# Hybrid diffusion trunk layer in split fp32: where three chores stand among the matmuls, and the column order of the routed token rows

## The reference, cut to what matters

```python
h = rmsnorm(x, g_pre1) * (1 + sc1) + sh1          # modulation rows from silu(c) @ w_mod + b_mod
proj = h @ w_in                                   # input projection, then RG-LRU and attention branches
t = (ga * out_a + gb * out_b) @ w_o               # output projection, 640 x 2048 @ 2048 x 2048
x = x + g1 * rmsnorm(t, g_post1)
h = rmsnorm(x, g_pre2) * (1 + sc2) + sh2
aff = softmax(h @ w_router)                       # 16 experts
vals, idx = top_k(aff.T, cap)                     # per expert 64 latent and 16 context tokens
xs = h[idx]
hid = silu(xs @ w_gate) * (xs @ w_up)
ye = (hid @ w_down) * vals                        # added back to the tokens' rows
x = x + g2 * rmsnorm(f, g_post2)
```

## Time and profile before

| what | value |
|---|---|
| median of 3 runs | 2970.52 us |
| lowest and highest run | 2968.2 and 2975.15 us |
| profiled execution | 2973.51 us |
| its span in the trace | 2971.9 us |
| PE busy | 2853.0 us (96%) |
| DVE busy | 2189.3 us (74%) |
| mean granted PE clock | 0.981 |

### The profile page before, as it was taken

One profiled execution on the slowest core, in us unless ns is written; L12 is line 12 of the kernel. 1 busy time (PEld: TensorE's weight loads), 2 busy tenths in 40 slices (PEclk: granted clock), 3 DMA queues, 4 the chain that ended last, 5 costly groups with the idle time before them and its releaser, 6 DMA issues.

```text
span 2971.9 us, 42745 instructions
## 1 busy us (share of the span) xinstructions
PE 2853.0 (96%) x15690; PEld 2303.6 (78%) x15690; DVE 2189.3 (74%) x1948; ACT 1555.7 (52%) x1510; POOL 287.3 (10%) x341
## 2 busy tenths in 40 slices
PE   7999999999999999999999996999999999999994
PEld 3689999999999999989988774666666666666662
DVE  7639688796777777763343567888888888888886
ACT  7821212224555555542232445777777777777774
POOL 1000000002111111000000000001000101101100
PEclk8999999999999999999999997999999999999997
DMA  9668677684333333364343656999999999999996
GB/s 380 245 214 257 203 251 236 210 278 124 120 118 119 118 119 119 98 196 130 115 143 125 253 200 235 355 383 395 377 394 379 391 386 376 382 377 383 384 392 236
DMA packets 293047, 757.51 MB, mean 255 GB/s; under 512 B 20328, under 2 KB 184720, under 8 KB 228320
## 3 DMA queue, kind: packets, MB, share of 16 engines
q1 hardware_dynamic: 267168, 639.52, 59.4%
q0 software_dynamic: 23264, 101.24, 10.6%
q10 hardware_dynamic: 2544, 15.82, 1.3%
HBM read 700.61 MB, written 55.89 MB: 255 GB/s over the span
## 4 chain that ended last, share of the span: by engine, by line
PE 80%; DVE 9%; issue 4%; DMA 4%; ACT 2%; DVEq 0%; SPq 0%; ACTq 0%; POOLq 0%; POOL 0%
PE ps L483 16%; PE ps L484 16%; PE ps L485 15%; PE ps L2077 7%; PE ps L2078 7%; PE ps L2079 7%; DVE mod_acc L1419 4%; PE ps L2211 2%; PE ps L2213 2%; PE ps L2212 2%; PE ps L1981 2%; PE ps L2141 1%; DVE probs L1640 1%; DMA raw<-in_w_mod 1%; DVE w_lo L438 1%
## 5 line engine op out<-in xcount | busy, mean ns | idle before, releaser
L416 DVE TENSOR_TENSOR we_lo<-raw,we_hi 128x2048 fp32r<-128x2048 f32 x384 | 876.3, 2290 | 137.4 <-ACT we_hi L411 137.2
L411 ACT ACTIVATE we_hi<-raw 128x2048 fp32r<-128x2048 f32 x384 | 736.9, 1919 | 285.1 <-PE ps L485 285.1
L2077 PE MATMUL ps<-hi,w_lo 128*128 128x320 f32 x2048 | 641.2, 313 | 4.3 <-DVE w_lo L387 4.3
L2079 PE MATMUL ps<-hi,w_hi 128*128 128x320 f32 x2048 | 632.8, 309 | 0.0
L2078 PE MATMUL ps<-lo,w_hi 128*128 128x320 f32 x2048 | 632.7, 309 | 0.0
L387 DVE TENSOR_TENSOR w_lo<-raw,w_hi 128x2048 fp32r<-128x2048 f32 (+1 forms) x120 | 272.7, 2273 | 204.0 <-ACT w_hi L377 198.8
L484 PE MATMUL ps<-we_lo,xs_hi 128*80 128x512 f32 x1024 | 402.6, 393 | 0.0
L483 PE MATMUL ps<-we_hi,xs_lo 128*80 128x512 f32 x1024 | 402.0, 393 | 0.1
L2077 PEld LDWEIGHTS ps<-hi,w_lo 128*128 128x128 f32 x2048 | 384.6, 188 | 20.7 <-issue 16.2
L485 PE MATMUL ps<-we_hi,xs_hi 128*80 128x512 f32 x1024 | 399.9, 391 | 0.0
L2078 PEld LDWEIGHTS ps<-lo,w_hi 128*128 128x128 f32 x2048 | 384.7, 188 | 0.2
(11 more groups left out here) (385 smaller groups left out, 3946.3 us busy)
## 6 DMA issues: line engine op xcount, KB each, us to landing
raw<-in_w_e_gate SPq DMA_DIRECT2D x128, 1024.0 KB, 7.1
raw<-in_w_e_up SPq DMA_DIRECT2D x128, 1024.0 KB, 7.6
raw<-in_w_e_down SPq DMA_DIRECT2D x128, 1024.0 KB, 12.1
raw<-in_w_in SPq DMA_DIRECT2D x144, 512.0 KB, 5.3
mod_raw<-in_w_mod SPq DMA_DIRECT2D x64, 1024.0 KB, 5.4
raw<-in_w_mod SPq DMA_DIRECT2D x64, 512.0 KB, 6.3
raw<-in_w_o SPq DMA_DIRECT2D x64, 512.0 KB, 4.7
d_proj<-stage POOLq DMA_DIRECT2D x32, 320.0 KB, 3.5
```

What stands on the lines that cost most here:

```text
L411: act.activation(we_hi[:, k % NEH, :], raw_slot(k), ACT.Copy).then_inc(hi_ready, 2)
L416: TTn(we_lo[:, k % NEH, :], raw_slot(k), we_hi[:, k % NEH, :].bitcast(F32), ALU.subtract).then_inc(lo_ready, 2)
L2077: pe.matmul(out, wl, hi[:, k, ms], start=(k % 16 == 0), stop=False)
L2079: last = pe.matmul(out, wh, hi[:, k, ms], start=False, stop=(k == KT - 1))
```

## The change

Nothing is added to or removed from what is computed. Five things move.

1. On PE the second pass's 16 turns and its router are cut into quarters. One quarter stands behind each k tile of a unit: turns in unit 2 and router in unit 3 for c = 0, in units 1 and 2 for c = 1 and 2. `halves_used` is raised at the unit's last matmul, ahead of the last quarter. The turn of the affinities moves a unit or two later.
2. ACT and DVE lists of the second pass are reordered to match: the first `split_hi` and `split_lo` stand ahead of the first root, `residual` of tile c+1 comes a block earlier, `affinities` is cut in two around a unit's `split_lo`.
3. `second_scale` and `second_shift` read their inputs at every second column and write `h2` with even columns first and odd columns behind. `turn_xs` then reads 128 adjacent columns.
4. In an expert, turns of `xs` blocks 4 to 7 stand between the two halves of `hid`; blocks 8 to 15 stay behind them.
5. `mod_row2` stands in unit n = 1 instead of n = 0.

```diff
             for u in range(32):
                 g, n = u // 8, u % 8
                 split_lo(dve, Q_IN + u // 4, u % 4 + 1)
-                if n == 0 and g:
+                if n == 1 and g:
                     mod_row2(g - 1)
...
+                if ps_ == 0:
+                    split_lo(dve, Q_O + 4, 1)
                 wait(dve, "rs1_sqrt", ps_ + 1)
...
+            def even_odd(x):
+                return x.rearrange("t (j q) -> t j q", j=2)
+
+            def by_parity(x):
+                return x.rearrange("t (q j) -> t j q", j=2)
...
-                own.done(STT(h2[:, q % 2, :], t_out[:, t, :], stats[:, 56 + t:57 + t], VL[:, 1, :], ALU.mult, ALU.mult))
+                own.done(STT(even_odd(h2[:, q % 2, :]), by_parity(t_out[:, t, :]), stats[:, 56 + t:57 + t],
+                             by_parity(VL[:, 1, :]), ALU.mult, ALU.mult))
...
-                TTn(h2[:, q % 2, :], h2[:, q % 2, :], shift[:], ALU.add).then_inc(S["h2_ready"], 1)
+                h = even_odd(h2[:, q % 2, :])
+                TTn(h, h, by_parity(shift[:]), ALU.add).then_inc(S["h2_ready"], 1)
...
+            residual(0)
+            split_lo(dve, Q_O + 4, 2)
+            second_scale(0)
+            split_lo(dve, Q_O + 4, 3)
+            second_shift(0)
+            residual(1)
+            split_lo(dve, Q_O + 4, 4)
+            evict(1, 0)
...
-                last.then_inc(halves_used, 2)
+                    if kk == 3:
+                        last.then_inc(halves_used, 2)
+                    if amid is not None:
+                        amid(kk)
...
+            def amid_second(c, kq):
+                turns_at, routes_at = (2, 3) if c == 0 else (1, 2)
+
+                def amid(kk):
+                    if kk == 0 and (c, kq) in ((1, 2), (2, 0), (3, 0)):
+                        turn_affinities(c - 1)
+                    if c < 3 and kq == turns_at:
+                        turn_x2_group(c, kk, 4 + kk % 2)
+                    if c < 3 and kq == routes_at:
+                        router_quarter(c, kk)
+
+                return amid
...
-                    xs = E["xs"][0:CAP, k // 2 * 2 * P + k % 2:(k // 2 + 1) * 2 * P:2]
-                    last = turn(ps[:, b + 1 + k // 6, n * CAP:(n + 1) * CAP], xs, CAP)
+                    at_ = k % 2 * (D // 2) + k // 2 * P
+                    last = turn(ps[:, b + 1 + k // 6, n * CAP:(n + 1) * CAP], E["xs"][0:CAP, at_:at_ + P], CAP)
...
                     last.then_inc(S["hidT_done"], 1)
+                    if h == 0 and not last_one:
+                        turn_xs(b_, range(4, 6), True)
+                        turn_xs(b_, range(6, 8), False)
                 if not last_one:
-                    turn_xs(b_, range(4, 6), True)
-                    turn_xs(b_, range(6, 12), True)
+                    turn_xs(b_, range(8, 12), True)
                     turn_xs(b_, range(12, 16), True)
```

More of the change, by code:

```diff
@@ L1772, in affinities @@
                 TS(sm[:, 1:2], sm[:, 0:1], -1.0, None, ALU.mult).then_inc(S["logit_max"], 1)
+            def affinities(q):
                 dve.wait_ge(S["logit_exp"], q + 1)
@@ L2240, in _, with o_unit @@
             leave(pe)
-            def o_unit(ps_, c, kq):
+            def o_unit(ps_, c, kq, amid=None):
                 b, n = o_banks(ps_, c)
@@ L2284, in router, with turn_x2_group @@
-            def router(q):
-                if q == 0:
+                    if kk == 3:
+                        last.then_inc(halves_used, 2)
+                    if amid is not None:
+                        amid(kk)
+            def turn_x2_group(q, g, bank):
+                if g == 0:
+                    pe.wait_ge(S["x2_ready"], q + 1)
+                    if q == 0:
+                        pe.wait_ge(S["o_taken"], 12)
+                    if q == 3:
+                        pe.wait_ge(S["o_taken"], 20)
+                if g >= 2 and q < 3:
+                    pe.wait_ge(S["x2T_taken"], 4 * q + g - 1)
+                elif g < 2 and 0 < q < 4:
+                    pe.wait_ge(S["x2T_taken"], 4 * q - 1 + g)
+                elif g >= 2 and q == 4:
+                    pe.wait_ge(S["x2T_taken"], 13 + g - 2)
+                for k in range(4 * g, 4 * g + 4):
+                    last = turn(ps[:, bank, (k % 4) * P:(k % 4 + 1) * P], t_out[:, ORDER[q], k * P:(k + 1) * P])
+                last.then_inc(S["x2T_done"], 1)
@@ L2286, in router, with router_quarter @@
+            def turn_x2(q, banks):
+                for g in range(4):
+                    turn_x2_group(q, g, banks[g])
+            def router_quarter(q, g):
+                if q == 0 and g == 0:
                     wait(pe, "swr_ready", 1)
-                for k in range(KT):
-                    if k % 4 == 0:
-                        pe.wait_ge(S["x2T_taken"], 4 * q + k // 4 + 1)
+                pe.wait_ge(S["x2T_taken"], 4 * q + g + 1)
+                for k in range(4 * g, 4 * g + 4):
```

107 lines of the change are left out of this document (53 added, 54 removed).

## The result

The changed kernel takes 2948.4 us (median of 4 runs, 2946.77 to 2950.69); the kernel before took 2972.68 us in the same measurement. The ratio is 0.9921, with a 95% interval of 0.9909 to 0.9933: faster by some 23 us (20 to 27) by the ratio, and by 24.3 between the medians. The profiled execution took 2947.37 us, its span is 2945.8 us (before 2973.5 and 2971.9), so 26.1 us are there to be found in the two traces. They lie as follows; the borders are starts of instructions in the timelines of PE and DVE.

The account below looks back on a forecast made before the run. PE, busy in 2853 of 2972 us, was taken as the bound. Second pass 12.5, experts with the first turns 11.9 and modulation row 1.7 sum to 26.1 us, giving 2944.5 us against the median; range 2938 to 2955.

Parts of the forecast that it names:

- The second pass: Second pass's column blocks: divided turns and routers and reordered chores gain 13.1 us by the terms, kept as 12.5.
- the breaks: Second pass: 24 added changes between large and small products cost 0.1 us each, 2.4 us (1 to 5).
- The clock's term: Stretches behind the second pass's three routers: no fall of the clock expected, so 5.9 us come back.
- the term for the rest: Second pass: 2.7 us of excess for restarts behind waits and the second router's slower end.
- The experts: From last up to first down matmul: 1.9 us against 2.67, 0.75 us an expert, 15 times, 11.3 us.
- the path of `hid`: In an expert, first down matmul waits for first half of `hid_lo`: 1.55 us behind four turns (0.3), 1.85 us.
- The first 16 turns: First expert's 16 `xs` turns, alone on the path: adjacent columns save 0.04 us each, 0.6 us.
- The modulation row: Input projection: moving `mod_row2` ends DVE's chain 0.6 us earlier a group, 1.7 us of PE's 4.3 (0 to 4.3).
- Strided DVE: Ten DVE instructions in and behind the second pass read every second fp32: cost taken as 0, 4.7 us kept.
- the rival: Strided reads slow DVE, some 1.36 us a row: 4.7 us behind the pass, 2949; chance 0.11.
- The loads: Experts' DMA: a period shorter by 1.1% asks 1.1% more; nothing given back, at worst all 11 us.
- that the mixed work holds the clock down: Second pass: blocks run at 0.5 from first quarter to end, 38 us and 2 for chores, 2990; chance 0.02.

Follow-up runs that it names:

- the experiment with the pass alone: The kernel before with only the second pass's new lists for PE, ACT and DVE: 2959.7 us, ratio 0.9958.
- the kernel with the undivided router: The change whole, but each of the second pass's three routers is one run of 32 products behind its unit: 2951.06 us, ratio 0.9929.
- without eight of the turns: The change whole, but the last 8 of an expert's 16 xs turns stand behind the first down unit: 2954.48 us, ratio 0.9945.
- at every eighth value: The change, but xs turned from every fourth column and second-pass scale and shift reading every eighth value: 2958.94 us (one run).

## Why the prediction was right

The forecast was 2944.5 us, in a range of 2938 to 2955; measured were 2948.4. The direction and the mechanisms held. Against the profiled execution, which was the sum's own measure, 26.1 us were forecast and the span is 26.1 us shorter. That this fits so closely is luck, as the terms show: the pass gave 2.1 us more than forecast and the other terms 2.0 less, and had the profile before caught one fall of the clock in its pass, as two other profiles of the same pass did, the difference would have been some 23. The medians of the measurement differ by 24.3.

- **The second pass: forecast 12.5, measured 14.6.** The mechanism is as told: clock 1.00 (the experiment with the pass alone has nearly the same windows), no wait for the copies, one of 0.2 us for `w_lo` in block 1 where I had put 0.3. The sum's terms came to 13.1 before I cut them, and the term that was mis-sized is the breaks: 24 of them were put at 0.1 us, 2.4 in all. The three blocks are 82.7 us; three times 21.9 of matmuls and 15.8 of chores leave 1.2 us, of which 0.2 is the wait, so a break costs about 0.04 us, my lower bound. (This is an estimate that takes the chores at their old price; the kernel with the undivided router gives some 0.06.) The 0.6 us that I held back for restarts was not needed either. The clock's term was 5.9 us because its windows began behind the routers; with what the falls cost inside them it is 6.8, and the difference stood in the term for the rest, so the sum is the same. One reason was too strong: that an undivided router makes the clock fall. It did so behind 9 of 15, and with this very pass behind one of three in two profiles, so the old pass loses 3.4 to 6.8 us to the clock. A forecast from one of those two profiles would have had some 3 us less to give back.
- **The experts: forecast 11.3, measured 10.6.** The place takes 1.96 us where I had put 1.92 (2.67 less 0.75). That the path of `hid` would end the place was right: without eight of the turns it is as long. That the turns would end near the same time was not: a turn is cheaper than I had it (0.066 to 0.07 us), so they are done some 0.18 us before, and the path is longer (1.95 us for 1.85).
- **The first 16 turns: forecast 0.6, measured 0.** 2.40 us against 2.41. They run at a clock of 0.50 behind 8.3 us of idle PE; there, adjacent and every second column cost the same (a load takes 230 ns either way). The 0.04 us came from rows at 1.00. This step of the prediction failed: a duration was carried over from one clock to another.
- **The modulation row: forecast 1.7, measured 1.2** on average over eleven profiles, 1.0 between these two (each wait 1.0 to 1.2 us, where 0.7 to 1.0 was to be seen), since the second tile's landing costs DVE 0.56 us instead of 0.2. (The sum's own 0.6 us three times is 1.8, not 1.7.) By the medians it can't be told from nothing.
- **Strided DVE: forecast 0, measured 0.** 2.35 us a row. The way in which the rival was priced was sound: at every eighth value the rows do stretch, and the stretch behind the pass grew by nearly their excess less the slack. Its 1.36 us a row was never met; at every eighth value it was 1.6 on average.
- **The loads: nothing given back, as forecast.** An expert's period went from 69.05 to 68.4 us, with DMA busy all of it and no wait of PE for a load.

Of the rivals, that the mixed work holds the clock down fell at once: each block has a clock of 1.00, with quarters of turns and of routers between six matmuls. The Trainium skill (TensorE: Matmul & The Clock Gate, section Part 4: PE-mode transpose) would have turns not count as PE activity; in no stretch read here did turns cost the clock, neither four at a time between matmuls nor 24 in a row (1.96 to 2.67 us) between the up and the down matmuls. Behind the second pass the traces say more. PE idles for 4.7 us there and then does nothing but 32 turns, and the clock rises in the midst of them (timeline of PE, after):

```profile
1767.27 5.24 PE L2025 MATMUL ps<-ident,t_out 128*128 128x128 f32 x32 [4.68 <-DVE t_out L1756]
```

Two windows inside that row:

```profile
1767.10:1770.40 3.30, 3.13 (x15) 3.13 (x16) 3.13 (x4) 3.12 (x5) 0.00 (x0) 0.50 0.99 417
1770.50:1772.60 2.10, 2.01 (x19) 1.77 (x17) 2.06 (x2) 2.10 (x4) 0.00 (x0) 1.00 0.53 218
```

It rises within these 32 turns in all fourteen profiles. So fp32 turns alone bring the clock back, and that sentence of the Trainium skill does not hold for them here.

## What to carry to other kernels

A long run of short products was best cut into pieces of under a microsecond and put between large matmuls: the breaks cost 0.04 to 0.06 us each, a fall of the clock 1.7 to 3.4. For the turns the case is weaker (0.8 us of waits, 1.3 us of the pass), as no run of turns cost the clock. Where a loss comes in some profiles and not in others of the same code, as the clock's here, a difference of two profiles is no measure of what an edit gave: look for it in every profile that has that code. Two edits that end at the same place do not add: before summing, find which path (here 1.96 us of multiply, turn, copy, subtract) stays when the work beside it is gone. When an engine falls behind by a little in each unit (here 1.7 us), look for where its backlog is reset by a wait, and put the lighter unit behind that reset and ahead of the one that is late.

## What the runs showed of the hardware that I had not expected

- A weight load of PE on fp32 pays once for columns that are not adjacent: 140 ns adjacent, 223 at every second, 217 at every fourth. DVE pays nothing at every second value (2.35 us) and 3.9 to 4.5 us at every eighth.
- At a clock of 0.50 the 16 turns of `xs` take 2.40 us from adjacent columns and 2.41 from every second one, 0.13 us from start to start, and a load takes 230 ns in both: the stride's price disappears there.
- 3.5 us of router products cost the clock in the first block (0.50 for 5.51 us behind it) and not in the second and third, in the same execution and with no wait ahead of any of them; and in two pairs of kernels with one and the same pass they cost it behind all three routers or behind the third alone. In pieces of 0.81 us they never did (27 routers).
- The clock rose from 0.50 to 1.00 while PE did nothing but fp32 turns (the 32 behind the second pass, in every profile).
